# Three reorderings in a hybrid retention and forgetting-attention step on one core: a weight load and the forget gate's products at the first strip, and retention's low halves

## What is computed

```
xn = rmsnorm(x)                        z = xn @ w_in        (rq rk rv rg fq fk fv ff ga gb)
logf  = log_sigmoid(ff + b_forget)     (8 columns of w_in: the forget gate)
ret_o = silu(rg) * groupnorm(retention(rotary(rq), rotary(rk), rv))   4 heads, chunked state
fox_o = softmax(fq fk^T + cumsum(logf) differences, causal) fv        8 heads
m     = sigmoid(ga) * (ret_o @ w_ret_out) + sigmoid(gb) * (fox_o @ w_fox_out)
h     = x + m @ w_o ;   y = h + relu(rmsnorm(h) @ w_ff1)^2 @ w_ff2
```

## Time and profile before

| | |
|---|---|
| median of three runs | 2173.83 us (2172.04 to 2173.98) |
| the profiled execution | 2172.89 us, span of its instructions 2171.2 us |
| mean granted clock of TensorE | 0.994 of full speed |
| busy share of the span | PE 98%, weight loads of PE 92%, DVE 50%, ACT 25%, POOL 3% |
| moved by DMA | 199.78 MB, mean 92 GB/s |

### The profile page before, as it was taken

The page is one execution under the profiler, slowest core; times in us unless marked ns, Lnnn a source line. Parts: engine busy times, 40 slices in busy tenths (PEclk is TensorE's granted clock), DMA queues, the critical chain, the costliest instruction groups (busy, mean ns, idle before and its releaser), DMA issues.

```text
span 2171.2 us, 31090 instructions
## 1 busy us (share of the span) xinstructions
PE 2128.0 (98%) x12606; PEld 1990.0 (92%) x12606; DVE 1077.9 (50%) x2207; ACT 541.6 (25%) x1103; POOL 57.4 (3%) x102
## 2 busy tenths in 40 slices
PE   7799999999999999999999999999999999999998
PEld 5688888889998899989989999999999999999998
DVE  4445632266666666665565635663333333333343
ACT  4533200022222222221142314341211212122130
POOL 1000000000000000000000000000000000000000
PEclk9899999999999999999999999999999999999999
DMA  5322232433232333236435453001111111111112
GB/s 190 104 80 78 84 120 80 139 121 105 90 115 67 124 124 105 90 124 221 141 118 159 155 166 91 26 26 58 49 39 49 49 46 42 49 49 40 49 39 81
DMA packets 187218, 199.78 MB, mean 92 GB/s; under 512 B 9600, under 2 KB 156744, under 8 KB 187088
## 3 DMA queue, kind: packets, MB, share of 16 engines
q1 hardware_dynamic: 173728, 148.85, 22.4%
q0 software_dynamic: 13360, 49.05, 5.9%
HBM read 144.50 MB, written 53.37 MB: 91 GB/s over the span
## 4 chain that ended last, share of the span: by engine, by line
PE 93%; DVE 4%; ACT 1%; DMA 1%; issue 1%; SPq 0%; ACTq 0%; DVEq 0%
PE ps_mlp L317 38%; PE ps_dense L317 24%; PE ps_mlp L339 18%; PE ps_out L987 4%; PE ps_scores L956 3%; PE ps_turn L940 2%; PE ps_scores L1032 1%; PE ps_turn L933 1%; PE ps_scores L1038 1%; PE ps_scores L1037 1%; DVE w_lo L304 1%; ACT act_hi L374 0%; PE ps_turn L938 0%; DMA w_raw<-in_w_in 0%; DVE act_lo L380 0%
## 5 line engine op out<-in xcount | busy, mean ns | idle before, releaser
L317 PE MATMUL ps_dense<-act_hi,w_lo 128*128 128x352 f32 (+2 forms) x1152 | 384.6, 334 | 0.6 <-DVE gated L1712 0.6
L317 PE MATMUL ps_dense<-act_hi,w_hi 128*128 128x352 f32 (+2 forms) x1152 | 384.2, 333 | 0.0
L317 PE MATMUL ps_dense<-act_lo,w_hi 128*128 128x352 f32 (+2 forms) x1152 | 383.7, 333 | 0.0
L317 PE MATMUL ps_mlp<-act_hi,w_lo 128*128 128x352 f32 x864 | 280.8, 325 | 0.0
L317 PE MATMUL ps_mlp<-act_lo,w_hi 128*128 128x352 f32 x864 | 279.0, 323 | 0.0
L317 PE MATMUL ps_mlp<-act_hi,w_hi 128*128 128x352 f32 x864 | 278.5, 322 | 0.0
L293 ACT CAST w_hi<-w_raw 128x1024 fp32r<-128x1024 f32 x128 | 133.6, 1045 | 472.1 <-PE ps_mlp L317 283.3
L317 PE MATMUL ps_mlp<-u_hi,w_lo 128*128 128x352 f32 x768 | 248.1, 323 | 0.0
L317 PE MATMUL ps_mlp<-u_lo,w_hi 128*128 128x352 f32 x768 | 246.4, 321 | 0.0
L317 PE MATMUL ps_mlp<-u_hi,w_hi 128*128 128x352 f32 x768 | 246.1, 320 | 0.0
L317 PEld LDWEIGHTS ps_dense<-act_hi,w_hi 128*128 128x128 f32 x1152 | 217.3, 189 | 4.9 <-issue 1.6
(11 more groups left out here) (281 smaller groups left out, 3112.3 us busy)
## 6 DMA issues: line engine op xcount, KB each, us to landing
w_raw<-in_w_in SPq DMA_DIRECT2D x65, 512.0 KB, 4.6
w_raw<-in_w_ff SPq DMA_DIRECT2D x64, 512.0 KB, 3.9
gates<-stage POOLq DMA_DIRECT2D x24, 528.0 KB, 3.5
stage<-gates SPq DMA_DIRECT2D x16, 528.0 KB, 3.7
negc_rows<-neg_cumsum SPq DMA_DIRECT2D x8, 792.0 KB, 7.5
rotated<-stage POOLq DMA_DIRECT2D x8, 536.0 KB, 3.0
fox_out_T<-fox_stage POOLq DMA_DIRECT2D x8, 528.0 KB, 4.8
ret_gate_T<-gates SPq DMA_DIRECT2D x8, 528.0 KB, 4.4
```

Source lines behind the costliest of these rows:

```text
L317: mm = nc.tensor.matmul(bank(n)[:, 0:w], lhs[:, k, m0:m0 + P], rhs[:, k, c:c + w], start=(x == 0), stop=(x == 3 * kc - 1))
```

## The change

On SP, unit 5 is loaded ahead of the wait for the row copies' stores, and unit 6 between that wait's first part (`a_lo`) and its second (`xst_out`). On PE, the forget gate's products go ahead of the spread, and tile 0 of strip 1 goes ahead of spread part 2. On DVE, the runs of eight low halves of rows are cut into runs of two to four, with retention's reads in between; `split(2)` of head 2 moves from chunk 0 to chunk 4; at the last group the first product's bank is read in the middle of the run, and its addition (`gated_add`) follows the run.

```diff
-    def resplit_lo(dve, j, src, base):
+    def resplit_lo(dve, j, src, base, ks=range(KC)):
         c, w = O3[j]
-        for k in range(KC):
+        for k in ks:
...
-        if j == 2:
+        if j == 2 and KC - 1 in ks:
             dve.wait_ge(a_lo, base + 3 * KC)
...
+        strip_units(1, (0,))
         sp.wait_ge(a_lo, A_NORM1)
+        strip_units(1, (1,))
         sp.wait_ge(xst_out[0], 16 * 5)
         sp.wait_ge(xst_out[1], 16 * 4)
...
-        for s in range(1, STRIPS):
+        strip_units(1, (2, 3))
+        for s in range(2, STRIPS):
             strip_units(s)
...
         pe.wait_ge(xst_ok, 2 * NQ)
+        pe.wait_ge(w_lo_s, U_FF + 1)
+        for j, (c, w) in enumerate(T3):
+            turned_step(pe, At(N_FF + j), ring(At(U_FF)), c, w)
         pe.wait_ge(dg_ok, 1)
         spread_scale(0)
         spread_scale(1)
-        pe.wait_ge(w_lo_s, U_FF + 1)
-        for j, (c, w) in enumerate(T3):
-            turned_step(pe, At(N_FF + j), ring(At(U_FF)), c, w)
+        strip_step(pe, 1, 0)
         spread_scale(2)
...
-            for i in range(NQ):
+            for i in range(1 if s == 1 else 0, NQ):
                 strip_step(pe, s, i)
...
+        def gated_add(n, m, w):
+
+            dve.wait_ge(bank_free, (n + 1).v)
+            nc.vector.tensor_tensor(m, m, mtmp[:, n.mod(2), 0:w], ALU.add).then_inc(m_ok, 1)
...
             ret_ad(r, 0)
-            split(2)
-            for c in range(1, NCH):
+            if r.first == 2:
+                resplit_lo(dve, 1, m_rows, A_NORM1, range(2, 5))
+                ret_ad(r, 1)
+                resplit_lo(dve, 1, m_rows, A_NORM1, range(5, KC))
+                ret_bd(r, 0)
+                read(0)
+                ret_ad(r, 2)
+                resplit_lo(dve, 2, m_rows, A_NORM1, range(4))
+                ret_bd(r, 1)
+                resplit_lo(dve, 2, m_rows, A_NORM1, range(4, KC))
+            else:
+                split(2)
+            for c in range(3 if r.first == 2 else 1, NCH):
                 ret_ad(r, c)
-                if c == 1 and r.first == 2:
-                    resplit_lo(dve, 2, m_rows, A_NORM1)
                 if c in (3, 6, 9):
                     read({3: 1, 6: 3, 9: 5}[c])
                 ret_bd(r, c - 1)
                 if c in (1, 4, 7):
                     read({1: 0, 4: 2, 7: 4}[c])
+                if c == 4 and r.first == 2:
+                    split(2)
...
             if r.first == 1:
-                resplit_lo(dve, 1, m_rows, A_NORM1)
+                resplit_lo(dve, 1, m_rows, A_NORM1, range(2))
...
-        resplit_lo(dve, 2, ret_rows, A_FOX)
+        resplit_lo(dve, 2, ret_rows, A_FOX, range(4))
+        gated(At(N_RET), 9, 0, mT[:, 0, 0:O3[0][1]], *O3[0], False, add=False)
+        resplit_lo(dve, 2, ret_rows, A_FOX, range(4, KC))
+        gated_add(At(N_RET), mT[:, 0, 0:O3[0][1]], O3[0][1])
...
-                gated(At(N_RET + 3 * q + j), 9 + q, q % 2, mT[:, q, c:c + w], c, w, False)
+                if q or j:
+                    gated(At(N_RET + 3 * q + j), 9 + q, q % 2, mT[:, q, c:c + w], c, w, False)
```

More of the change, by code:

```diff
@@ L1702, in ret_bd, with gated @@
             dve.wait_ge(r_bd, r.times(NCH, c + 1))
-        def gated(n, gate_count, slot, m, c, w, first):
+        def gated_add(n, m, w):
+            dve.wait_ge(bank_free, (n + 1).v)
+            nc.vector.tensor_tensor(m, m, mtmp[:, n.mod(2), 0:w], ALU.add).then_inc(m_ok, 1)
+        def gated(n, gate_count, slot, m, c, w, first, add=True):
             dve.wait_ge(g_ok, gate_count)
@@ L1712, in gated @@
             nc.vector.tensor_tensor(mtmp[:, n.mod(2), 0:w], z, gt, ALU.mult).then_inc(bank_free, 1)
-            dve.wait_ge(bank_free, (n + 1).v)
-            nc.vector.tensor_tensor(m, m, mtmp[:, n.mod(2), 0:w], ALU.add).then_inc(m_ok, 1)
+            if add:
+                gated_add(n, m, w)
         def ret_head(r, fox):
```

## The result

Four runs of the changed kernel lie between 2148.19 and 2153.79 us, with a median of 2151.77; the kernel before beside them has 2173.78. The ratio is 0.9903, with a 95% interval of 0.9891 to 0.9916. The forecast was 2154.1 in a range of 2150.8 to 2158.6. The profiled execution is the shortest of the four, 2148.19 us, with a span of 2146.4. A second set on another occasion gave 2150.70 (2149.71 to 2154.27) against 2172.62 before, 0.9907 (0.9890 to 0.9923).

What follows compares the result with a forecast made beforehand. PE is busy 98% of the span, so only its waits and lower clock can give time: 14.6 (first strip) + 4.5 (head 2) + 0.6 (last group) = 19.7 us, a predicted median of 2154.1, range 2150.8 to 2158.6.

Steps and rivals of the forecast that it cites:

- First strip: Behind strip 0 on PE: the 12.16 us idle for diagonal tiles and 2.43 of slow clock go, 14.6 us.
- no unit load took over 8.7: Strip 1's loads: units 6 and 7 reckoned at 8.7 us each, so no wait in tile 0, margin 1.3.
- The chain that the prediction gave for unit 8: Strip 1: unit 8 loads at unit 6's low half, 86.1, lands at 90.9, done at 93.2; needed at 94.5.
- The two edits pay for the same idle: First strip: without the early load, tiles would come at 89.69 against products ending at 89.3; with it, at 80.5.
- Head 2: Retention on PE: 4.34 us of idle become 1.55, and 1.7 of slow clock goes, 4.5 us, bounds 0 to 6.0.
- the new waits: Head 2 on PE: read(0) waits for the first gate's sigmoid, so 0.85 us at ret_b(2) and 0.7 at piece 6.
- the reason I gave for no fall: Head 2: the two new waits together are shorter than the 1.87 us pause, behind which the clock stayed 1.00.
- Last group: PE's idle before the first gated read goes as the run of eight low halves is split, 0.6 us.
- The clock did not fall in head 2: Rival, chance 0.2: the new waits in head 2 bring the lower clock, so it gives 2.8 us; 2155.8 us.
- head 2 gave its share: Rival, chance 0.1: head 2 gives nothing, as DVE has as many instructions as before; 2158.6 us.
- the weights were not late: Rival, chance 0.04: strip 1's weights come far too late, PE waits in tile 0; unit 8 at 117 gives 2179.0.
- the early load that does not do what it says: Rival, chance 0.08: unit 8 stays at 97.3 behind the tables, PE waits 2.8 us in tile 0; 2156.9 us.

Runs made afterwards that it cites:

- before_again: The kernel before, unchanged, profiled once more: the clock fell again in head 2, to 0.80 behind a pause of 2.14 us.
- after_again: The changed kernel, unchanged, timed a second time beside the kernel with head 2's first read later: median 2150.70 us, 0.9907 of the kernel before.
- first_strip_back: The changed kernel with SP's order, products behind the spread and tile 0 behind part 2 all as before; retention stays changed: 2165.85 us.
- read_later: The changed kernel with read(0) of head 2 one place later on DVE, behind ret_ad(2) and four low halves: 2150.92 us.
- tile_after: The changed kernel with tile 0 of strip 1 back behind spread part 2: 2151.44 us.
- runs_of_eight: The changed kernel with head 2's low halves back in two runs of eight and split(2) back in chunk 0: 2153.71 us.
- after: The changed kernel itself, as first measured against the kernel before: median 2151.77 us, ratio 0.9903.
- runs_of_eight_2: A second run of the changed kernel with head 2's runs of eight and split(2) in chunk 0 back: retention's stage 234.25 us.
- read_later_5: The changed kernel with read(0) of head 2 one place later on DVE, timed four times: median 2149.26 us, 0.9892 of the kernel before.

## Why the prediction was right

**First strip, 14.6: measured 14.7** (14.2 between before_again and after_again). The products start at once, the clock stays at 1.00, nothing waits in tile 0. first_strip_back takes just this back. The step behind it was the weak one: "no unit load took over 8.7". Unit 7 went out at 75.63 behind the tables and its high half started at 87.00, 11.4 us later. The timelines of DVE and PE show unit 8's low half and the first matmul that needs it:

```profile
90.67 1.21 DVE L304 TENSOR_TENSOR w_lo<-w_raw,w_hi 128x1024 fp32r<-128x1024 f32 x1
```

```profile
92.12 0.39 PE L339 MATMUL ps_mlp<-w_lo,act_hi 128*128 128x512 f32 x1
```

It was done at 91.88, a margin of 0.2 instead of 1.3, in an execution where PE was early. The chain that the prediction gave for unit 8 was wrong in two places, with errors of opposite sign. Unit 6's low half was done at 78.46 + 1.22 = 79.7 instead of 86.1, so unit 8's load left 6.4 us sooner than reckoned, of which 2.5 is the earlier start of this execution. But unit 8's low half then stood on DVE behind unit 7's, which waited for the long load. That no wait came of it is partly luck, though it held in all nine profiles of kernels with these loads. In read_later, where PE was 2.8 us later, unit 7 went out at 78.39 and its high half started at 86.65, 8.3 us later; in tile_after it took 8.9. So the same place in the queue gave 8.3 to 11.4 us, and a load that changes its neighbours must not be given the time that it had among the old ones.

**The two edits pay for the same idle: right.** 9.6 and 9.9 alone, 14.7 together. The prediction put the tiles at 89.69 against products that end at 89.3, so 0.4 us for the diagonals without the early load, and 0.46 was measured. The bracketed waits alone would have put the kernel with one edit 3 us from the changed one; with the clock behind them it was 5. In both of these kernels tile 0 stayed ahead of spread part 2.

**Head 2, 4.5: measured 4.5, and the new waits 1.24 + 0.24 against 0.85 + 0.7.** The place (`ret_b(2)`, piece 6) and the cause (read(0) waits for the gate's sigmoid) were as forecast, and read_later shows the cause by taking it away. The sum was right in its two halves too: 2.9 for the order of DVE's work, from runs_of_eight against after, and 1.7 for the clock, which only the kernel before paid. That the 1.7 belongs to the edit is less sure than the 2.9: the kernel before paid it in both its profiles, but the kernel with the runs of eight back had the same pauses and paid it in neither: once the clock did not fall, once the fall was hidden. What does not hold is the reason I gave for no fall, that the pause of 1.87 had left the clock alone: in runs_of_eight_2 that same pause lowered it to 0.58. A length of pause below which the clock is safe can't be read off one trace. The Trainium skill, TensorE: Matmul & The Clock Gate, section "HAM oscillation — how this bites in real kernels", tells of a kernel whose waits for data let the lower rate back in each time, so that a pause is paid again in slower matmuls; its waits are longer than the 1.55 us to which the prediction applied it. The trace agrees where the clock fell (about 1.7 us each time), and adds that a fall is free where another engine sets the end of the stretch.

**Last group, 0.6: mis-sized.** The edit is worth 0.8 from start to start, since the bracket that the prediction took for the gain understates the pause, and the profile's 1.2 has 0.4 of a pitch that changes between executions.

**The sum.** 14.7 + 4.5 + 0.8 = 20.0 where 19.7 was forecast. The medians differ by 22.0 and 21.9. The 2 us that are left are partly luck of the draw: over all the timed runs on record, 20 of the kernel before (mean 2172.4) and 8 of the kernel after (2151.4), the means differ by 21.0. In the profiles the rest lies in the two columns that no edit moves, strip 0's end (74.5 to 77.6) and the end (846.7 to 849.9). One kernel shows both ends of either range there, as runs_of_eight and runs_of_eight_2 do; whether the changed kernel meets the shorter ones more often was not settled.

**The rivals.** The clock did not fall in head 2 after the change; head 2 gave its share; the weights were not late. The one that came nearest is the early load that does not do what it says: 0.2 us from its first effect.

## What to carry to other kernels

When two edits attack one idle time, reckon what each leaves, and count with the clock's price behind a rest of some 2 us (five of the six pauses of 2.1 to 2.9 us told of here had it): the second edit may be worth more than the few us that it still finds. Cut the two traces at instructions that both have, and compare stage by stage: retention repeated to a tenth of a us here and the two other stages to about half a us, while the whole time of one kernel moved by 6. When work is cut into short runs to let an engine's urgent steps through, look for waits for other engines' results among the short runs, and place them late enough that the result is there.

## What had not been expected of the hardware

The start and the end of the program vary by about 3 us each, with one kernel. The windows of the first stretch, before and after, show the start: the clock was 0.89 in one and 1.00 in the other, and PE got through 33 and 46 instructions of the same list.

```profile
8.00:24.00 16.00, 10.79 (x33) 8.40 (x34) 8.06 (x10) 7.17 (x11) 1.89 (x2) 0.89 1.03 361
```

```profile
8.00:24.00 16.00, 10.68 (x46) 8.35 (x46) 9.32 (x12) 8.80 (x14) 2.45 (x3) 1.00 1.03 364
```

In all fourteen profiles of the table, the changed kernel's as well as the other's, the first column is 74.5 to 75.3 where this clock is 1.00 and 76.9 to 77.6 where it is 0.89. (It leaves something out: in both executions the first matmuls from 10.8 on had a pitch of 0.43 us, where 0.23 is usual, up to 13.96 after and 15.70 before.)

At the end it is the landing of the last stores. PE's waits in the kernel with unit 7 ahead, against 1.1 us as the longest for `y_rows` in the kernel after:

```profile
PE ps_turn L1159 <- DVE y_rows L1943: 3.7, 3, 2.7
```

The chains that ended last, in the kernel after and in this one, each hold one of these stores and the eight transposes behind it:

```profile
2138.82 2.61 DMA out<-y_rows
...
2142.31 1.08 PE ps_turn L1158 x8
```

```profile
2138.03 4.22 DMA out<-y_rows
...
2143.11 1.94 PE ps_turn L1159 x8
```

So the late store costs 1.6 us and the lower clock behind the pause (0.50 from 2143.00 to 2147.20) about as much again. In every profile one or two of the nine last stores land late (in 3.2 to 5.1 us, where 1.9 to 2.6 is usual), and which ones decides the last column: 846.7 to 847.0 where it is the fourth (in the kernel after it took 4.93 us, and PE did not wait for it), 849.2 to 849.9 where it is the fifth and sixth, 848.1 to 848.6 where it is a later one. Two executions of one kernel differ in this (read_later and read_later_5, for one), so no edit of this document decides it; why a store is late is open.

And 500 matmuls of one form, with no pause among them and a granted clock of 1.00, took 80.18 us in some executions and 80.55 in others, 0.5% more.
